# Eleven table units made beside the second feed-forward's output product, and a root ahead of transfers

## The reference, cut to what matters

```python
h = h + 0.5 * rmsnorm(swiglu(rmsnorm(h, ffn1_pre_w), ffn1_w_gu, ffn1_w_down), ffn1_post_w)
u = rmsnorm(h, mix_pre_w)
h = h + rmsnorm(token_mixing(u, ...), mix_post_w)
h = h + 0.5 * rmsnorm(swiglu(rmsnorm(h, ffn2_pre_w), ffn2_w_gu, ffn2_w_down), ffn2_post_w)
# second block, x = h
k_ctx, v_ctx = context_kv(modulate(ctx, norm1_g, ch1, cs1), p)
x = x + g1 * token_mixer(modulate(x, norm1_g, sh1, sc1), p, attend)   # ends in "merged @ w_out"
x = x + g2 * peer(modulate(x, norm2_g, sh2, sc2), p)
# peer: act = gelu(x . u_tab[idx]); out = (gate * act) . v_tab[idx]
```

## Time and profile before

| | us |
|---|---|
| median of 3 runs | 3959.32 (3954.81 to 3963.67) |
| the profiled execution's own time | 3960.99 |
| its span | 3959.2 |
| PE busy in it | 3575.9 (90%) |
| first gate stage | about 40 to 328 |
| first output product | 334 to 467 |
| second output product | 1541 to 1676 |
| wout2 | 2415 to 2464 |

### The profile page before, as it was taken

The page is one execution under the profiler, slowest core; times in us unless marked ns, Lnnn a source line. Parts: engine busy times, 40 slices in busy tenths (PEclk is TensorE's granted clock), DMA queues, the critical chain, the costliest instruction groups (busy, mean ns, idle before and its releaser), DMA issues. The chain is left out here.

```text
span 3959.2 us, 50914 instructions
## 1 busy us (share of the span) xinstructions
PE 3575.9 (90%) x17547; PEld 3025.7 (76%) x17547; DVE 2267.8 (57%) x4241; ACT 1384.0 (35%) x2049; POOL 1706.8 (43%) x781
## 2 busy tenths in 40 slices
PE   8999898899899999968989999988888999988788
PEld 5777676677776787746776667788888999988788
DVE  4552336422333553176755554599999655667787
ACT  4332233322443322223232453233465433433332
POOL 5775332233333443322333113444323667656555
PEclk9999898999999999979999999998999999998989
DMA  7997853455564464313242126844356888878875
GB/s 249 383 387 252 271 159 119 139 165 159 172 207 152 144 191 132 93 52 117 91 129 90 59 74 224 319 134 131 129 184 235 307 309 326 314 293 321 306 292 218
DMA packets 427310, 794.62 MB, mean 201 GB/s; under 512 B 28393, under 2 KB 293545, under 8 KB 407115
## 3 DMA queue, kind: packets, MB, share of 16 engines
q1 hardware_dynamic: 291104, 475.39, 35.9%
q10 hardware_dynamic: 117610, 182.91, 13.8%
q0 software_dynamic: 18432, 134.23, 8.9%
HBM read 673.40 MB, written 186.12 MB: 217 GB/s over the span
## 5 line engine op out<-in xcount | busy, mean ns | idle before, releaser
L535 POOL TENSOR_TENSOR weights_lo<-weights_raw,weights_hi 128x1024 fp32r<-128x1024 f32 x649 | 1580.3, 2442 | 2214.7 <-ACT weights_hi L1221 2208.0
L608 PE MATMUL bank<-operand_hi,weights_hi 128*128 128x512 f32 (+1 forms) x2856 | 1096.5, 384 | 63.6 <-DVE operand_lo L1899 23.4
L609 PE MATMUL bank<-operand_lo,weights_hi 128*128 128x512 f32 (+1 forms) x2856 | 1065.8, 373 | 0.0
L610 PE MATMUL bank<-operand_hi,weights_lo 128*128 128x512 f32 (+1 forms) x2856 | 1065.2, 373 | 0.0
L1221 ACT ACTIVATE weights_hi<-weights_raw 128x1024 fp32r<-128x1024 f32 x649 | 679.7, 1053 | 973.6 <-PE bank L610 643.2
L608 PEld LDWEIGHTS bank<-operand_hi,weights_hi 128*128 128x128 f32 x2856 | 542.8, 190 | 157.1 <-DVE operand_lo L1899 29.5
L609 PEld LDWEIGHTS bank<-operand_lo,weights_hi 128*128 128x128 f32 x2856 | 543.3, 190 | 74.8 <-issue 6.3
L610 PEld LDWEIGHTS bank<-operand_hi,weights_lo 128*128 128x128 f32 x2856 | 541.6, 190 | 75.4
L608 PE MATMUL bank<-expert_hi,weights_hi 128*128 128x384 f32 x1024 | 357.8, 349 | 91.2 <-POOL weights_lo L535 87.1
L609 PE MATMUL bank<-expert_lo,weights_hi 128*128 128x384 f32 x1024 | 354.0, 346 | 0.0
L610 PE MATMUL bank<-expert_hi,weights_lo 128*128 128x384 f32 x1024 | 352.6, 344 | 0.0
(11 more groups left out here) (397 smaller groups left out, 4881.8 us busy)
## 6 DMA issues: line engine op xcount, KB each, us to landing
weights_raw<-in_w_ffn_gu SPq DMA_DIRECT2D x132, 512.0 KB, 5.8
weights_raw<-in_w_peer SPq DMA_DIRECT2D x112, 512.0 KB, 6.2
expert_table<-expert_turned ACTq DMA_DIRECT2D x288, 128.0 KB, 4.9
expert_table<-in_w_peer_out SPq DMA_DIRECT2D x72, 512.0 KB, 5.4
weights_raw<-in_w_peer_ahead SPq DMA_DIRECT2D x72, 512.0 KB, 3.8
weights_raw<-in_w_peer_out SPq DMA_DIRECT2D x72, 512.0 KB, 6.3
expert_table<-in_w_peer SPq DMA_DIRECT2D x56, 512.0 KB, 5.4
expert_rows<-in_w_peer ACTq DMA_DIRECT2D x54, 512.0 KB, 6.9
```

The costliest lines, as they stand in the source:

```text
L535: pool.tensor_tensor(LO[:, slot, :], RAW[:, slot, :], HI[:, slot, :].bitcast(F32), ALU.subtract).then_inc(sem("lo_ready"), 1)
L608: pe.matmul(out, wh, hi(k), start=(k == 0), stop=False)
L609: pe.matmul(out, wh, lo(k), start=False, stop=False)
L610: ins = pe.matmul(out, wl, hi(k), start=False, stop=(k == kc - 1))
```

## The change

The table's units are dealt out anew: `f1` 46, `d1` 21, `f2` 18, `d2` 11, `q` 32. In the first gate stage pairs have three units and two by turns, five or six for a `two_pairs`, and DVE's loop over i is written out. Block 7 of the first output product has no units. In the second output product 11 units go through one rows buffer and one turned buffer, in SBUF that the gate stage no longer uses: one for each of blocks 0 to 6 ahead of the block's copy, and one more behind the copies of blocks 1, 2, 4 and 5 (behind the context's norm in block 1). ACT saves the latter at the beginning of the next block, after one split, and the former after the block's splits and ahead of its square. Before its first `d2` load ACT waits until the hidden values are complete. The first context block waits on DVE until the `d2` stores have landed. In wout2 the root comes ahead of the two last `save_rows`.

```diff
-TABLE = {"f1": range(0, 54), "d1": range(54, 78), "f2": range(78, 96), "q": range(96, 128)}
+TABLE = {"f1": range(0, 46), "d1": range(46, 67), "f2": range(67, 85), "d2": range(85, 96), "q": range(96, 128)}
+GATE_PAIRS = range(2, 20)
+DOWN2_MORE = (1, 2, 4, 5)
+def turns_of_pair(pair):
+    return 3 - (pair - GATE_PAIRS.start) % 9 % 2 if pair in GATE_PAIRS else 0
+def down2_turns(m):
+    return (1 if m < 7 else 0), (1 if m in DOWN2_MORE else 0)
...
+        URE = place("expert_rows_down2", [P, UNIT * P], F32, A0 + FC * 4096)
+        UTE = place("expert_turned_down2", [P, UNIT * P], F32, A0 + FC * 4096 + 4096)
...  (ACT, ffn)
-                        if s == 0 and 3 <= pair <= 20:
+                        if s == 0 and (pair - 1 in GATE_PAIRS if mix == 1 else turns_of_pair(pair - 1) == 3):
                             save_rows(which)
...
                     act.dma_start(CT[:], a["ctx"]).then_inc(sem("ctx_loaded"), 16)
+                    act.wait_ge(sem("hidden_ready"), 2 * FC)
+                    load_rows("d2")
                 issued = 0
                 for m in range(DC):
-                    units(units_by(m) - issued)
+                    more = units_by(m) - issued
+                    if name == "ffn2" and m and down2_turns(m - 1)[1]:
+                        units(1)
+                        more -= 1
+                        save_rows("d2")
+                    units(more)
                     issued = max(issued, units_by(m))
-                    if name == "ffn1":
+                    if name == "ffn1" and m < DC - 1:
                         for _ in range(3):
                             save_rows("d1")
+                    if name == "ffn2" and down2_turns(m)[0]:
+                        save_rows("d2")
                     square(YT[:, m, :], TOK, "block_free", n["freed"] + m + 1)
...  (ACT, blocks_and_squares)
                     square(src[:, m, :], TOK, "block_free", n["freed"])
+                    if m == DC - 1:
+                        root(TOK)
                     if table:
                         for _ in turns_at("wout2", m):
                             save_rows("q")
-                root(TOK)
...  (DVE, ffn)
+                    if k:
+                        turn_rows(which, p, lambda buffers: i - 1)
+                    elif c < turns_of_pair(2 * i + p):
+                        turn_rows(which, turned1[0])
+                        turned1[0] += 1
...
-                with dve.Fori(2, FC // 2 - 1) as i:
-                    two_pairs(i)
+                if k == 0:
+                    for i in range(2, FC // 2 - 1):
+                        two_pairs(i)
+                else:
+                    with dve.Fori(2, FC // 2 - 1) as i:
+                        two_pairs(i)
...
-                        for t in range(3 * m, 3 * m + 3):
+                        for t in range(3 * m, 3 * m + 3) if m < DC - 1 else ():
                             turn_rows("d1", t)
                         copy_blocks(YT, 1, FC, first=m, scaled=True)
...
-                    copy_blocks(YT, 2, FC, scaled=True)
+                    for m in range(2):
+                        turn_down(down2_turns(m)[0])
+                        copy_blocks(YT, 1, FC, first=m, scaled=True)
...  (the context's norm)
-                    copy_blocks(YT, DC - 2, FC, first=2, scaled=True)
+                    turn_down(down2_turns(1)[1])
+                    for m in range(2, DC):
+                        turn_down(down2_turns(m)[0])
+                        copy_blocks(YT, 1, FC, first=m, scaled=True)
+                        turn_down(down2_turns(m)[1])
...  (DVE, context_block)
+                if c == 0:
+                    dve.wait_ge(sem("table_stored_d20"), stored_into("d2", 0))
```

More of the change, by code:

```diff
@@ L146, in steps_of_group @@
     return (), ()
-TABLE = {"f1": range(0, 54), "d1": range(54, 78), "f2": range(78, 96), "q": range(96, 128)}
+TABLE = {"f1": range(0, 46), "d1": range(46, 67), "f2": range(67, 85), "d2": range(85, 96), "q": range(96, 128)}
[5 more added lines that the diff above has]
+    return (1 if m < 7 else 0), (1 if m in DOWN2_MORE else 0)
+assert sum(map(turns_of_pair, GATE_PAIRS)) == len(TABLE["f1"])
+assert sum(sum(down2_turns(m)) for m in range(8)) == len(TABLE["d2"])
 WOUT_TURNS = 9
@@ L242, in program, with stored_into @@
         UTD = [place(f"expert_turned_down{i}", [P, UNIT * P], F32, x_at + 24576 + 4096 * i) for i in range(2)]
+        URE = place("expert_rows_down2", [P, UNIT * P], F32, A0 + FC * 4096)
+        UTE = place("expert_turned_down2", [P, UNIT * P], F32, A0 + FC * 4096 + 4096)
         URW = [place(f"expert_rows_q{i}", [P, UNIT * P], F32, A0 + 49152 + 4096 * i) for i in range(4)]
         UTW = [place(f"expert_turned_q{i}", [P, UNIT * P], F32, A0 + 65536 + 4096 * i) for i in range(4)]
-        ROWS = {"f1": (UR, UT), "d1": (URD, UTD), "f2": (UR[:2], UT), "q": (URW, UTW)}
+        ROWS = {"f1": (UR, UT), "d1": (URD, UTD), "f2": (UR[:2], UT), "d2": ([URE], [UTE]),
+                "q": (URW, UTW)}
+        def stored_into(which, i):
+            into = len(ROWS[which][1])
+            return 64 * len(range(i, len(TABLE[which]), into))
         YT = place("branch_out", [P, DC, TOK], F32, x_at)
@@ L550, in gather @@
                     for which in TABLE:
-                        into = len(ROWS[which][1])
-                        for i in range(into):
-                            pool.wait_ge(sem(f"table_stored_{which}{i}"), 64 * len(TABLE[which]) // into)
+                        for i in range(len(ROWS[which][1])):
+                            pool.wait_ge(sem(f"table_stored_{which}{i}"), stored_into(which, i))
                     pool.wait_ge(sem("best_ready"), TT)
@@ L1957, in ffn @@
                 mix = 1 if k else 2
-                which, each = ("f2", 1) if k else ("f1", 3)
+                which = "f2" if k else "f1"
+                turned1 = [0]
                 def turn(i, p, c):
-                    t = each * p + c
-                    turn_rows(which, t, lambda buffers: 2 * each // len(buffers) * (i - 1) + t // len(buffers))
+                    if k:
[3 more added lines that the diff above has]
+                        turned1[0] += 1
                 def two_pairs(i):
@@ L1968, in two_pairs @@
                         for o, buffer in enumerate(UT):
-                            dve.wait_ge(sem(f"table_stored_{which}{o}"), 64 * len(TABLE[which]) // 2)
+                            dve.wait_ge(sem(f"table_stored_{which}{o}"), stored_into(which, o))
                     for p in range(2):
@@ L1976, in two_pairs @@
                             turn(i, p, 0)
-                            if each > 1:
+                            if k == 0:
                                 turn(i, p, 1)
@@ L1987, in two_pairs @@
                                           ALU.subtract).then_inc(sem("hidden_ready"), 1)
-                        if table and each > 1:
+                        if table and k == 0:
                             turn(i, p, 2)
@@ L2013, in ffn, with turn_down @@
                 else:
-                    copy_blocks(YT, 2, FC, scaled=True)
+                    turned2 = [0]
+                    def turn_down(count):
+                        for _ in range(count):
+                            turn_rows("d2", turned2[0])
+                            turned2[0] += 1
+                    for m in range(2):
+                        turn_down(down2_turns(m)[0])
+                        copy_blocks(YT, 1, FC, first=m, scaled=True)
                     n["square"] += 1
```

5 lines of the change are left out of this document (3 added, 2 removed).

## The result

The changed kernel takes 3940.26 us (median of 5 runs, 3927.22 to 3940.59) against 3961.77 for the kernel before (5 runs, 3954.81 to 3963.67): a ratio of 0.9939, 95% interval 0.9923 to 0.9955. Timed again later, 5 runs against 9 of the kernel before (3959.20), it took 3931.37, a ratio of 0.9934 (0.9920 to 0.9948). The profiled execution took 3940.59, its span is 3938.8, 20.4 shorter than before.

What follows compares the result with a forecast made beforehand. PE, busy 90% of the span, was taken to bound the kernel. Terms -3.6 - 10.3 - 4.0 + 3.5 = -14.4 against the median 3959.32 gave 3945 us; range 3937 to 3954, by the terms' bounds 3940 to 3951.

Steps and rivals of the forecast that it cites:

- First gate stage, -3.6: First gate stage: eight fewer units and a written-out loop bring DVE's copy sooner, removing fold waits; 3.6 us gained, bounds 0 to 4.0.
- no wait over 0.1 us: First gate stage: sign that the forecast holds, no wait of the fold (L801) over 0.1 us.
- End of the first output product, -10.3: End of first output product: without units in block 7 the seam shrinks by 10.3 us, bounds 9 and 10.5.
- The first two terms: End of first output product: PE's wait before the last sum 7.20 to 0.59 us, sum to `mean_square` 2.11 to 1.16.
- the table load hides beside the sum: End of first output product: third term, reciprocal 1.39 us after `mean_square` instead of 4.34, 2.95 us gained.
- wout2, -4.0: End of wout2: root ahead of ten transfers brings the reciprocal 4.55 us sooner; 4.0 us gained after 0.5 given back.
- The half microsecond to be given back: End of wout2: ten transfers issued behind the root for 5.8 us delay the first operand's high part, costing 0.5 us.
- The drain: Both root seams: the skill counts 1.38 us more per table load, making the total 1.4 us smaller; the prediction took none.
- Second output product, +3.5: Second output product: 11 units through one buffer of each kind delay PE at step 8 of block 4, costing 3.5 us.
- three rings: Second output product: each ring, four stores issued (2.2), load (5.4) and turn (1.25), takes 8.9 us; three precede save 4.
- rival (a): Second output product: loads land in 4.3 us, so the ring is hidden and the total is 3941 us; chance 0.15.
- First output product, 0: First output product ahead of its end: earlier blocks keep their three units and PE's stalls there stay; no change.

Runs made afterwards that it cites:

- waits first: The kernel after with ACT's two waits for stores moved ahead of block 7's square in the first output product; span 3936.9 us.
- root first: The kernel before with only wout2's root issued ahead of the last transfers; 3965.45 us against 3966.07 for the kernel before beside it.
- loop written out: The kernel before with only DVE's loop over the first gate stage written out, 54 units staying there; span 3954.6 us.
- block 7 back: The kernel after with three units put back beside block 7 of the first output product and three fewer beside the second; span 3951.1 us.
- before repeated: The kernel before, unchanged, traced again; span 3952.7 us against 3959.2 in its first trace.
- after repeated: The kernel after, unchanged, run again; 3931.37 us, ratio 0.9934 to the kernel before, span 3929.6 us.
- 13 units: The kernel after with 13 units, not 11, beside the second output product and two fewer in the last stages; span 3955.0 us.

## Why the prediction was right, step by step

**First gate stage, -3.6: right, a little small.** -4.5 against the first trace of before, and -4 to -8 against its three; eight traces with the new stage lie within 0.5 us (292.5 to 293.0). The eight folds of the earlier trace rows are on time, 4.0 us; the ninth, which the window of those rows left out, waits its 1.7 us as before, so the sign "no wait over 0.1 us" failed there. By difference the fewer turns and their order carry most; the written-out loop had been given nothing, and got 1.0 in the traces without half clock.

The working left out one thing that made the folds late. In the turn of the earlier trace rows DVE's cast took 1.90 us and not 0.43, and ended 0.3 us after POOL had ended its low parts; without that the copy would be 1.5 us sooner, more than the turn's 1.25. From 60 to 320 in the traces of the old stage, 17 or 18 of DVE's 38 casts and low parts are drawn out in this way, each ending 0.28 to 0.55 us behind a low part of POOL, 30.5 us in all in the first. With the loop alone written out it is 14 and 24.4 us, in the kernel after 2 and 4.2 us. Before, DVE then POOL (two of its low parts in one row); after, DVE:

```profile
219.61 1.90 DVE L1984 CAST hidden_hi<-gate_silu 128x512 f32 x1
```

```profile
216.46 4.75 POOL L535 TENSOR_TENSOR weights_lo<-weights_raw,weights_hi 128x1024 fp32r<-128x1024 f32 x2
```

```profile
214.84 0.43 DVE L2022 CAST hidden_hi<-gate_silu 128x512 fp32r<-128x512 f32 x1
```

So the gain came by the forecast's way, an earlier copy, but how much of it is the turn that went and how much the casts that are no longer drawn out was not tried apart.

**End of the first output product, -10.3: -9.2.** The first two terms are right (PE's wait 0.58, the sum to `mean_square` 1.16). The failed term is the third, "the table load hides beside the sum". It cost (2.75 - 1.39) = 1.36. What held the load was `mean_square`, as its row says, and not the stores: these had landed by 459.7, 8 us before it. In this program a wait for stores between the square and the root puts the load behind the root's own wait as well; where nothing stands between them (wout2, and waits first), the load follows the square at once and the root alone waits. Waits placed ahead of the square gave 1.2 of it back. There the square, behind the same waits, began 0.17 us after the copy's end and in the kernel after 0.04, so the waits held it by 0.13 at most.

**wout2, -4.0: -4.57**, shown alone and in the whole. The half microsecond to be given back was not: eight stores and two loads were issued in 4.9 us and not 5.8, so ACT was free as the first operand came.

**The drain.** The root follows its load by 0.02 us in the kernel after (468.13, 1.28 long, 469.43), and in wout2 the load follows the square by 0.02 (2449.64, 0.63 long, 2450.29). The Trainium skill's extra 1.38 us (ScalarE: Activation LUTs, What ACT_TABLE_LOAD costs) is not there in these rows either.

**Second output product, +3.5: +0.4.** Place and step were right, the size was not. The prediction put three rings at 26.7 us; from save 1 (1576.54) to save 4 (1600.11) they took 23.6, and those 3.1 us are the error. The ring's load was taken at 5.4 and its stores at 2.2. In these three rings the loads landed in 3.9, 6.2 and 3.9 us, 4.7 on the mean, and the stores were issued in 1.8 to 1.9. This is near rival (a), whose landing was 4.3; the median of 5.1 over the whole stage hides it. The Trainium skill's fit for GpSimd's path (DMA: Bandwidth & Descriptors, Anatomy of one DMA) gives 3.2; none of the 128 loads of table rows in the kernel after landed under 3.4.

**First output product, 0: +2.8, not the change's.** The stall at its start was in the page of before and I passed over it, since the change left it. The dip of the clock behind it comes and goes. The product takes 131.7 to 132.2 us in traces without a dip there (before, root first, loop written out, block 7 back), 133.1 to 133.8 with 3.4 us of half clock (before repeated, after repeated, waits first), and 134.9 to 135.0 with 6.8 (after, 13 units).

**The sum.** The four terms make -17.7 (-4.45 - 9.16 - 4.57 + 0.46) where -14.4 was forecast; most of the difference is the ring. The first pair of traces differs by 20.4. The rest stands in stretches whose code is the same: +2.8 in the first output product and -3.3 in the attention stage (7.9 less the 4.6 of the root), both with the half clock, and -2.2 spread over the others, among them 0.6 ahead of the first reciprocal.

The timed differences, 21.5 and 27.8 us by the medians, are larger than 17.7. Their intervals, 17.8 to 30.5 and 20.6 to 31.7, both lie above it, the first by a tenth. If the gate stage is put at the mean of its traces, it is 5.8 and not 4.5. The repeats of before and after, a second pair, differ by 23.1: 18.6 in the four changed places (5.2, 9.4, 4.4, less 0.4), and 3.7 in a stretch that the table does not show, from the first output product's reciprocal to the second output product. Its code is the same, and it takes 1059 to 1060 us in eight traces, with 78 to 82 us of half clock, and 1055 to 1057 in four, with 72 to 74. Of the 27.8 a part stays open.

That the median of 3940.26 fell into 3937 to 3954 is in part luck: the terms' errors are -0.9, +1.1, -0.6 and -3.0 us and cancel in part, and the second timing, 3931.37, lies under the range. The prediction's own range by the bounds of its terms is also too narrow: 0, 9 and 2 us gained and 7.7 lost give 3956, not 3951.

## What to carry to other kernels

When DMA work is dealt out beside dense work, what counts is less how much of it there is than what stands behind it on the issuing engine: the same three units cost 9.5 us beside the last block of one output product (15.25 against 5.74) and 0.4 beside the middle blocks of the other. Between the last square and the root put no wait that the root itself doesn't need: here it put the table load behind `mean_square`. Put it where the engine idles anyway. A gain of some us out of thousands is shown by the stretch between two instructions, over several traces; a single time can hide it, as that of the moved root did.

## What the runs showed of the hardware

The stall of 2.8 to 3.7 us at the start of the first output product came with half clock in five of nine traces, of the same code in part; the clock fell between 1.2 us before the stall's end and 0.9 behind it. With the stall removed there was none in three of three. Its length doesn't decide it: 3.39 had none, 2.81 had some. PE has run between 0 and 6.8 us at the lower level, for 0 to some 3 us of time.

DVE's cast of 128x512 took 0.43 us, in some turns beside a low part of POOL too, and in others up to 2.7 us. Every cast drawn out in this way ended 0.28 or 0.29 us after a low part of POOL had ended. The counts stand with the gate stage above.

The last stage took 856.1 to 869.6 us with the same instructions. In the two windows above the granted clock is 0.96 and 0.94, which is 75.1 us of half clock against 99.0, and the second is 12 us longer. PE's busy time is 7.0 of these and its idle time 5.0, so the clock is the larger part but not all. The first trace of before and the repeat of after have the same 82 us of half clock in this stage and take 862.6 and 856.1 us: there PE waits 91.2 and 83.4 us in it, nearly all of it for POOL's low parts. Most of the scatter between executions of one kernel lies here, and not in any change.
